# Gate and up products of a SwiGLU stage as seven block products in place of eight, inside a one-core hybrid encoder step

## The reference, cut to what matters

```python
h  = x + concat(pool_out, attn_out) @ w_out          # (2048 + 64 rows, 1024)
hn = rms_norm(h, norm_ffn)                           # the second norm
y  = h + (silu(hn @ w_gate) * (hn @ w_up)) @ w_down  # w_gate, w_up: 1024 x 2816; w_down: 2816 x 1024
```

## Time and profile before

| | |
|---|---|
| median of 3 runs | 2290.54 us (2288.74 to 3587.15) |
| profiled execution | 2290.56 us, its span 2288.8 us |
| granted TensorE clock | 0.998 of full speed |
| PE busy | 2223.7 us (97%), 12667 matmuls |
| PEld busy | 1997.5 us (87%) |
| DVE busy | 956.7 us (42%), 1685 instructions |
| ACT busy | 759.3 us (33%) |
| POOL busy | 642.5 us (28%), 296 instructions |

### The profile page before, as it was taken

The page is one execution under the profiler, slowest core; times in us unless marked ns, Lnnn a source line. Parts: engine busy times, 40 slices in busy tenths (PEclk is TensorE's granted clock), DMA queues, the critical chain, the costliest instruction groups (busy, mean ns, idle before and its releaser), DMA issues.

```text
span 2288.8 us, 32450 instructions
## 1 busy us (share of the span) xinstructions
PE 2223.7 (97%) x12667; PEld 1997.5 (87%) x12667; DVE 956.7 (42%) x1685; ACT 759.3 (33%) x1601; POOL 642.5 (28%) x296
## 2 busy tenths in 40 slices
PE   7999999999999999999999999999999899999999
PEld 6876799999999989767999999999887689999998
DVE  3558713322222255586222332222566753434244
ACT  4575422121121235764312112111357442222221
POOL 2410332223223214112332323223141224333331
PEclk9999999999999999999999999999999999999999
DMA  4110231212112133002321212211331223223221
GB/s 135 47 38 1 93 111 56 73 55 73 55 55 75 37 122 109 19 19 92 93 70 59 73 55 66 62 56 56 102 107 38 82 74 102 83 75 90 73 74 42
DMA packets 194378, 159.97 MB, mean 70 GB/s; under 512 B 7005, under 2 KB 176906, under 8 KB 194282
## 3 DMA queue, kind: packets, MB, share of 16 engines
q1 hardware_dynamic: 191326, 149.58, 21.3%
q10 hardware_dynamic: 2956, 9.08, 1.0%
HBM read 149.66 MB, written 9.07 MB: 69 GB/s over the span
## 4 chain that ended last, share of the span: by engine, by line
PE 83%; DVE 8%; ACT 5%; issue 2%; POOL 1%; DMA 1%; SPq 0%; DVEq 0%; ACTq 0%; POOLq 0%
PE ps L597 26%; PE ps L599 26%; PE ps L598 26%; DVE s_sb L1479 2%; ACT s_sb L1107 2%; DVE negmax L1484 1%; DVE xn L1343 1%; PE ps L694 1%; PE ps L732 1%; POOL w_lo L501 1%; PE ps L710 1%; DVE h L1355 1%; DVE kt_sb L1402 1%; PE ps L611 1%; DVE xt_lo L1331 1%
## 5 line engine op out<-in xcount | busy, mean ns | idle before, releaser
L501 POOL TENSOR_TENSOR w_lo<-raw,w_hi 128x1024 fp32r<-128x1024 f32 x249 | 596.9, 2417 | 1497.9 <-ACT w_hi L980 863.1
L597 PE MATMUL ps<-xt_hi,w_hi 128*128 128x384 f32 (+1 forms) x2640 | 859.4, 326 | 2.9 <-issue 1.8
L599 PE MATMUL ps<-xt_hi,w_lo 128*128 128x384 f32 (+1 forms) x2640 | 852.8, 323 | 0.0
L598 PE MATMUL ps<-xt_lo,w_hi 128*128 128x384 f32 (+1 forms) x2640 | 852.5, 323 | 0.0
L597 PEld LDWEIGHTS ps<-xt_hi,w_hi 128*128 128x128 f32 x2640 | 497.7, 189 | 10.7 <-issue 4.9
L598 PEld LDWEIGHTS ps<-xt_lo,w_hi 128*128 128x128 f32 x2640 | 497.8, 189 | 2.6 <-issue 0.3
L599 PEld LDWEIGHTS ps<-xt_hi,w_lo 128*128 128x128 f32 x2640 | 497.4, 188 | 0.0
L1355 DVE TENSOR_TENSOR h<-ps,h 128x512 f32<-128x512 f32 (+1 forms) x510 | 348.7, 689 | 239.0 <-PE ps L599 237.4
L1567 DVE TENSOR_TENSOR aa<-ps,sg 128x384 f32<-128x384 f32 (+1 forms) x132 | 69.2, 524 | 823.7 <-PE ps L599 821.9
L1202 ACT ACTIVATE sg<-ps 128x384 f32<-128x384 f32 (+1 forms) x132 | 61.3, 464 | 663.1 <-PE ps L599 663.0
L597 PE MATMUL ps<-w_hi,act_hi 128*128 128x512 f32 x704 | 279.6, 397 | 0.0
(11 more groups left out here) (131 smaller groups left out, 1760.2 us busy)
## 6 DMA issues: line engine op xcount, KB each, us to landing
raw<-in_w_gate SPq DMA_DIRECT2D x66, 512.0 KB, 3.8
raw<-in_w_up SPq DMA_DIRECT2D x66, 512.0 KB, 4.0
raw<-in_w_down SPq DMA_DIRECT2D x66, 512.0 KB, 3.2
raw<-in_w_in SPq DMA_DIRECT2D x33, 512.0 KB, 4.0
raw<-in_w_out SPq DMA_DIRECT2D x24, 512.0 KB, 4.1
h<-in_x_prompt SPq DMA_DIRECT2D x16, 512.0 KB, 7.5
out<-h ACTq DMA_DIRECT2D x16, 512.0 KB, 2.7
xload<-in_x_prompt SPq DMA_DIRECT2D x10, 512.0 KB, 3.5
```

The costliest lines, as they stand in the source:

```text
L501: nc.gpsimd.tensor_tensor(lo, raw, hi.bitcast(F32), ALU.subtract).then_inc(done, 1)
L597: nc.tensor.matmul(out, w_hi, m_hi, start=first, stop=False)
L598: nc.tensor.matmul(out, w_hi, m_lo, start=False, stop=False)
L599: return nc.tensor.matmul(out, w_lo, m_hi, start=False, stop=last)
```

## The change: what it does

Gate and up are each one product of a 2 by 2 block matrix (feature half by k half) and a 2 by 2 block matrix (k half by row half). The change computes it with seven block products of 4 k-steps in place of eight, by sums of blocks ahead of it (four sums on the weights, four on the normed rows) and sums of the products behind it. A product is 12 matmuls, 14 products make a group.

- Weights: DVE adds and subtracts 128x512 blocks in `raw2` and the new tile `st` (`combine_weights`, four instructions for gate and four for up of every group; POOL does the first). The halves of each product's weight block go to one of four slots of a ring (`ring_hi`, `ring_lo`): ACT writes the high half when the product four places earlier is done (`high_product`), POOL the low half (`low_product`), each 128x512.
- PE: for group j the order is seven gate products (1, 6, 5, 7, 2, 3, 4), the down product of group j-1, seven up products. Products 2, 3 and 4 add onto a PSUM bank that another product left there. Group 0 has an order of its own with all 14 in a row.
- DVE sums the products (`sums`), multiplies (`gated`), and writes the low halves (`act_low`); `act_hi`, `act_lo` are now single.
- At the second norm, rows of tile pairs are combined (`combine_inputs`: POOL for pairs 0 and 1, DVE for pair 2), and 21 PSUM banks of transposes take the place of 12 (10 in part 2).
- Three buffers have moved or have become their own; the rows of the next part are loaded after products of the last group.

The core of the diff, in the order of the engines:

```diff
+ORDER = (1, 6, 5, 7, 2, 3, 4)
+GROUP = [(which, p) for which in range(2) for p in ORDER]
+GROUP0 = [(0, 1), (1, 1), (0, 2), (0, 6), (0, 5), (0, 7), (0, 3), (0, 4), (1, 6), (1, 5), (1, 7), (1, 2),
+          (1, 3), (1, 4)]
+SLOTS = 4
+DOWN_AT = (8, 9)
...
 # POOL
+            def low_product(which, product, q, number):
+                slot = q % SLOTS
+                low(left(which, product), ring_hi[:, slot], ring_lo[:, slot], split2, number)
...
+                    for n in range(PRODUCTS):
+                        target = n + SLOTS
+                        if target < PRODUCTS or not last:
+                            number = number + 1
+                            q = PRODUCTS * odd + target
+                            low_product(*(order + GROUP)[target], q, number)
+                        if n in DOWN_AT:
+                            number = number + 1
+                            low1(DOWN_ID + DOWN_AT.index(n), number)
...
 # PE
+            def product(s, j, odd, which, p):
...
+                pe.wait_ge(split2, RING2 * s.p + OUT2 + q + 1)
+                if p == 1 and not first:
+                    if which == 0:
+                        pe.wait_ge(a_done, s.g0 + 4 * j - 2)
+                    else:
+                        pe.wait_ge(silu_done, s.g0 + 4 * j + 2)
+                elif p == 2:
+                    pe.wait_ge(u1_done, m + 1)
+                elif p == 6:
+                    need(pe, u2_done, m)
+                elif p == 5:
+                    need(pe, c12_done, m)
+                elif p == 7:
+                    need(pe, c21_done, m)
...
+            def group(s, j, odd):
+                multiply(s, j, odd, 0)
+                down(s, j - 1, 1 - odd)
+                multiply(s, j, odd, 1)
...
+                for at, t in enumerate(s.order3):
+                    add_tile(s, s.d_unit(3, 0), 1, at, t, *out_operands(3))
+                    if at == 2:
+                        norm2_transposes(s, 0, B_BLOCKS[0:2])
+                    elif at == 3:
+                        norm2_transposes(s, 0, B_BLOCKS[2:3])
+                    elif at == 4:
+                        norm2_transposes(s, 0, T_BLOCKS)
+                norm2_transposes(s, 1, B_BLOCKS)
+                norm2_transposes(s, 2, B_BLOCKS[0:2])
...
+                    if n == 0:
+                        pe.wait_ge(tp_free, tp[0])
+                    elif n == 2:
+                        norm2_transposes(s, 1, T_BLOCKS)
+                    elif n == 3:
+                        norm2_transposes(s, 2, B_BLOCKS[2:3])
+                        norm2_transposes(s, 2, T_BLOCKS)
...
 # ACT
+            def first_partial(s, j, which):
...
+                act.wait_ge(prod_done, s.q0 + seq(j, which, 1) + 1)
+                if which == 0:
+                    need(act, a_done, s.g0 + 4 * j)
...
+            def group(s, j, odd, last=False):
...
+                    if p == 1 and not first:
+                        first_partial(s, j, which)
...
+                    if n + SLOTS < PRODUCTS:
+                        high_product(s, j, odd, *order[n + SLOTS])
...
+                    block = {7: (1, 1), 2: (0, 0), 3: (0, 1), 4: (1, 0)}.get(p)
+                    if block:
+                        (silu if which == 0 else act_high)(s, j, block)
...
 # DVE
+            def combine_weights(s, j, which):
...
+                dve.wait_ge(split2, low_done(s, j, 0, 3) if which else low_done(s, j - 1, 1, 3))
+                nc.vector.tensor_tensor(st[:, 0], b[:, 0:HALF], b[:, HALF:], ALU.add).then_inc(s_ready, 1)
+                dve.wait_ge(s_ready, 4 * m + 1)
+                nc.vector.tensor_tensor(st[:, 1], st[:, 0], a[:, 0:HALF], ALU.subtract).then_inc(s_ready, 1)
+                nc.vector.tensor_tensor(b[:, 0:HALF], a[:, 0:HALF], b[:, 0:HALF], ALU.subtract)\
+                    .then_inc(s_ready, 1)
+                dve.wait_ge(s_ready, 4 * m + 2)
+                nc.vector.tensor_tensor(st[:, 2], a[:, HALF:], st[:, 1], ALU.subtract).then_inc(s_ready, 1)
...
+            def group(s, j, odd, last=False):
+                for part in ("U2", "t", "C22", "C12", "C21"):
+                    sums(s, j, 0, part)
+                combine_weights(s, j, 1)
+                if not (isinstance(j, int) and j == 0):
+                    accumulate(s, OUT_GROUPS + j - 1, 1 - odd)
+                for part in ("U2", "t", "C22"):
+                    sums(s, j, 1, part)
+                gated(s, j, (1, 1))
+                if not last:
+                    combine_weights(s, j + 1, 0)
+                gated(s, j, (0, 0))
+                act_low(s, j, (1, 1))
+                sums(s, j, 1, "C12")
+                gated(s, j, (0, 1))
+                act_low(s, j, (0, 0))
+                act_low(s, j, (0, 1))
+                sums(s, j, 1, "C21")
+                gated(s, j, (1, 0))
+                act_low(s, j, (1, 0))
```

More of the change, by code:

```diff
@@ L109, in __init__ @@
         self.x0 = 2 * before
+        self.n0 = before + 2 * len(NT) * p
         self.z0 = 2 * len(SLABS) * p
@@ L859, in down, with multiply @@
+            def multiply(s, j, odd, which):
+                for p in ORDER:
+                    product(s, j, odd, which, p)
             def down(s, j, parity):
```

765 lines of the change are left out of this document (487 added, 278 removed).

## The result

The changed kernel takes **2406.46 us** (median of four runs, 2405.19 to 2408.78) where the kernel before takes 2290.11. The ratio is 1.051, 95% interval 1.050 to 1.053: slower by 116 us, as forecast. One of the runs of the kernel before was a slow one (3587.15 us) and is left out of the ratio. The sizes of the terms agree less well than their sum.

The account below looks back on a forecast made before the run. It took PE's matmul time (97% busy) to bound the kernel before. Terms -126.7 + 77 + 96 + 52 + 14 + 4 = +116 on 2290.6 us gave 2407 us, range 2300 to 2445, its own case at 0.57.

Parts of the forecast that it names:

- The mechanism: Loop: DVE and POOL alternate one instruction each, delaying the multiply before PE's next group; 2.8 us, part 2 6.3 us.
- Matmuls, -126.7: Gate and up products: 168 matmuls a group instead of 192, at unchanged spacing, save 126.7 us.
- Rival D: All 462 products: PE's spacing does not hold, a 0.1 us gap each, 46 us; no separate chance given.
- POOL's price, 1.29: POOL's 128x512 instruction takes 1.29 us, interpolated between trace rows of 256 and 1024 columns.
- Loop waits of parts 0 and 1, 3.9 us a group: PE waits 2.8 us for DVE's multiply and 1.05 us later; groups of 49.8 us, +77 us in total.
- Loop waits of part 2, +96: PE waits 6.3 us, then 1.4 and 1.9 us; groups of 45.1 instead of 38.7 us, ten passages.
- the second chain: Loop: later DVE work, then ACT, then POOL's ring half delay PE again; 1.05 us, part 2 1.4 and 1.9 us.
- Second norm, +52: ACT and DVE orders interlock, rounds of 5 to 7 us not 3.66; +18 in parts 0 and 1, +16 in part 2.
- group 0, +14: Group 0: no down product covers the up weight sums, so 4.6 us lie open, three times.
- Part end, +4: End of a part: the last down product waits 1.2 us for DVE's low halves.
- Rival A: POOL does not get between ready DVE instructions, or halves near 1.1 us; loop waits 2 and 6 us, 2334 us; chance 0.20.
- Rival B: Loops: POOL finishes its five instructions before DVE's weight sums, all loop waits go, 2234 us; chance 0.15.

Follow-up runs that it names:

- e3: Changed kernel with the four gate weight sums of groups 1 to 10 reading one input from PSUM, true sums left out; 2320.1 us.
- e6: Changed kernel with the down blocks' low halves moved from POOL to DVE beside the gate products, down blocks asked for last in a group; 2311.0 us.
- e10: Changed kernel with the down blocks' low halves kept on POOL but moved to the next group's gate products, down blocks asked for last; 2336.5 us.
- e4: Changed kernel with unread matmuls (9, in part 2 34) ahead of PE's wait at each group's first gate product; 2395.4 us.
- e5: Changed kernel with DVE adding both halves of a tile's output unit before scaling the previous tile at the second norm; 2395.8 us.
- e9: Changed kernel with down low halves on DVE, norm adds before scaling, ACT ring halves earlier, and three reorderings at second norm and group 0; 2262.1 us.

## Why the prediction was right, point by point

**The mechanism.** It was right: DVE's weight sums and POOL's five instructions meet in one stretch, by turns, and the multiply behind them holds PE's next group. e3 shows that the meeting is what costs (86 us go with it). e6 and e10 show that the down blocks in that stretch are its larger part. That the turns are strict is read from rows, not tested on its own.

**The sum, term by term.** From the starts of PE's matmuls in the two traces: matmuls -120 (forecast -126.7), waits and lowered clock in the loops of parts 0 and 1 +56 (+77) and of part 2 +75 (+96), second norm +70 (+52), group 0 +20 (+14), ends of the parts +16 (+4). The loops were forecast 42 us too high, all the rest 43 us too low. That the sum came out to the microsecond is luck; that the change is slower by more than 2% is not: had only one side been wrong, the time would have been some 2365 or 2450 us.

**Matmuls, -126.7.** A little too much. Groups of parts 0 and 1 without a wait measure 46.3 us where the spacing of the earlier trace rows gave 45.9; against 50.15 that is 3.85 us a group in place of 4.2. Rival D (0.1 us at each product) is thereby about 0.03 us a product. In part 2 no run had loops without a wait, but between waits the matmuls of the change start every 0.131 to 0.134 us, as in the earlier trace rows, so the 35.5 us stands. Waits as listed must not be taken off a group to find this: they count from the end of the matmul before, and from start to start each costs 0.16 to 0.17 us more.

**POOL's price, 1.29.** Right: 1.29 or 1.30 us where DVE is not in its way, means of 1.36 and 1.42 us with turns. The 1.11 us estimated from the Trainium skill (GPSIMD Engine Reference, Elementwise — side-by-side cycle accounting) was too low; the interpolation between two rows of the trace was the better source.

**Loop waits of parts 0 and 1, 3.9 us a group.** The first was 1.84 us, not 2.8: the turns held, but began earlier than laid out, since down block 0 is done (429.28) before DVE's multiply starts (429.69). The second (1.05 us at the fifth gate product) is not there. In its place stands the lowered clock, 1.4 us in 7 of 18 groups, which had no term. The rest, 0.4 us a group, is 0.17 us that each listed wait costs beyond its listed length (see above) and a slower spacing just behind it. Together 2.8 us over a floor that was 0.4 us higher: a group of 49.1 against the forecast 49.8. The waits were 1.1 us too large, the floor 0.4 us too small.

**Loop waits of part 2, +96.** 5.10 us in place of 6.3, and of the 1.4 and 1.9 us of the second chain at most 0.6 us shows as a wait, because PE runs at the lower clock (0.50) for a few us while the chain catches up, which costs some 2 us; e4 makes the chain visible (0.2 and 1.6 us). The group is 43.0 us, not 45.1: about 20 us too much in ten passages.

**Second norm, +52, and group 0, +14.** The interlock of ACT and DVE was there (e5), the wait in group 0 too: 4.30, 4.31 and 4.20 us against 4.6. But from output group 3 to the fourth product were 52.45 us, not 47.6, so +23 a part and not +18. Two steps failed. "POOL's sums for pair 0 end at about 18 and cost nothing": PE waited 3.43 us for them at 273.91, 19 us in, with the last tile's products ready behind. This is the smaller one: the first product starts 36.4 us in (forecast 35), and e9, which computes that tile first, brings it only 1.3 us further forward than e5 (from 31.7 to 30.3). The larger one is the stretch behind: from the first to the fourth product are 16.0 us, forecast 12.6. PE has the lower clock until 295.0, which had no term, and waits 1.3, 1.4 and 0.7 us for ACT's copy, DVE's sums and their low half. In e9, with pair 1's transposes a product earlier and the clock at 1.00, it is 12.3 us. In part 2 the whole is +24, not +16.

**Part end, +4.** The wait was as forecast, 1.21 us. Not seen: PE then works the boundary to part 1 with waits of 0.8, 0.6 and 2.5 us for DVE's additions; from the start of the last down product to the next first scores it takes 5.2 and 3.6 us longer than before.

**By part**, up to the first scores of part 1, from there to those of part 2, and from there to the end: +21, +20 and +74 us, forecast +17, +17 and +83.

**Rival A** (2 and 6 us of waits a group) is nearer in the loops than the case I held: they lost 2.8 and 7.5 us over their floors, where I had 3.9 and 9.6. Its reason was wrong all the same, since POOL does get in between DVE's instructions and its halves take 1.29 us, and in total it would have been off by 72 us, since the other terms are as low as mine. **Rival B** is worth a second look: with the two down blocks off POOL all loop waits of parts 0 and 1 go, as it said, but only when the kernel is written so (e6), not in the one as given. Even then it was not 2234: e6 is 23 us over the kernel before on its chip (2287.9), with parts 0 and 1 some 4 and 7 us shorter than before and part 2 32 us longer.

## What to carry to other kernels

Before counting the matmuls that an algebraic saving removes, lay its small sums beside what POOL does at that moment: instructions of 0.65 us with both inputs in SBUF took up to 2.88 us here, and where POOL's blocks stood was worth 70 us with the same work on the same engine. When a wait is removed and another appears at once, look for an instruction that needs nothing yet stands behind one that waits: on ACT such an order cost a wait of 1.3 us a group in part 2, and changing it made the group 1.0 us shorter. And price a fraction of the work (a part with fewer rows) by itself: PE's share shrinks with the rows, the weights' share does not, so that 74 of the 116 us came from the smallest part. And a sum of terms that comes out right is not yet terms that are right: compare them one by one.

## What the runs showed of the hardware

- After a PE wait of 1.2 to 1.9 us at the start of a group the granted clock fell in 8 of 20 cases (0.73, then 0.82 in the rows above) and stayed at 1.00 in the others; after 4.5 to 5.2 us it was at 0.50 each time (10 of 10, part 2). With unread matmuls in the wait (e4) it stayed at 1.00 in the loops.
- A 128x512 DVE instruction with two SBUF inputs that begins while a POOL instruction runs ends 0.55 us after POOL's does, whenever it began (80 of 80 weight sums in the change); alone it takes 0.64 to 0.68. With one input in PSUM it takes 0.68 to 0.69 beside POOL.
- At the same 384 columns and full clock, matmuls on `xt_hi`, `xt_lo` start every 0.177 us in seven products of a group, those on `tx` every 0.174 (e6, every group in parts 0 and 1). It is not the tile alone: the product right behind the down product also reads `xt_hi`, `xt_lo` and has 0.174. Why is open.
- A wait of PE listed as 1.84 us costs 2.01 us from start to start, since it is counted from the end of the matmul before, which overlaps the next when nothing waits.
